# Expert 0's input by a gather of six tiles and one-hot products for the last two, with its first weights split ahead

## The chip, the cores and the metric

One core of one Trainium2 chip runs the whole layer. The metric is the device time of one launch in microseconds (us), taken as the median of several runs. Its engines are TensorE (PE; PEld is its weight load), VectorE (DVE), ScalarE (ACT), GpSimd (POOL) and SyncE (SP), which issues most transfers.

## What is computed

One decoder layer on 1024 tokens of width 1024, in float32:

```python
xn   = rms_norm(x, norm_mix_w)
proj = xn @ w_in                      # b, c, h, q, k, v, 512 columns each
yc   = conv group, ya = stick-breaking attention (8 heads x 64)
x    = x + concat([yc, ya]) @ w_out   # the "projection" of this text
xf   = rms_norm(x, norm_ffn_w)
g_idx = argmax(xf @ w_group + b_group)             # 4 groups
top_v, top_i = top_k(expert logits of that group, 2)   # 2 of 8 experts
gate = softmax(group)[g_idx] * softmax(top_v)
h    = silu(xf[rows of e] @ w1[e]) * (xf[rows of e] @ w3[e])
out[rows of e] += gate * (h @ w2[e])               # for each of 32 experts
```

## The kernel before

**Stages.** The mixer (input projection, convolution, attention) takes the first 420 us or so. Then come the projection with w_out, which also makes the normed rows and the routing tile by tile (a tile is 128 tokens, m = 0 to 7), then 32 rounds, one for each expert, and at the end the combination of the two experts' rows for each token.

**Precision.** Every large product runs as three float32r matmuls: an operand is split into `hi` (ACT or POOL rounds it) and `lo` (DVE subtracts), and PE sums hi*hi, hi*lo and lo*hi. For an expert's weights ACT makes `e_hi` in four pieces of 128x1024 (`act_split`, L1192 of the profile) and DVE makes `e_lo` (`dve_split`, L1198); `pe_product` uses a piece with six matmuls (L1161 to L1163).

**Projection.** For each tile PE multiplies two halves of 512 columns (`multiply`; `mixed` counts the halves), DVE adds them to the residual (`add`, L1693), ACT squares and takes roots (`square`), DVE scales (`scale`, for the last tile `scale_last` in two halves, L1707), and SP stores the normed tile in the DRAM array `xn2_rows`. PE turns the residual rows (`turn`, L1458), ACT or DVE copies them out (`x2T`; for the last half DVE at L1849), PE multiplies them with the router's weights (`route`, L1468), and DVE chooses groups and experts (`bias`, L1717, to `chosen`, L1774).

**Ranks and table.** The rank of each pair of token and expert among the expert's pairs comes from products of `chosen` with triangular and all-ones matrices (`count_before`, L1479 and L1481, and `count_all`), for tiles in the groups 0-3, 4-5, 6 and 7. `rank` (from L1782) turns them into slot and column; `one_hots` makes two one-hot matrices for each of 16 steps, and `table` (L1492) sums their products in PSUM: entry (slot, expert) is the token's number. `slots` (L1803) reads the table when all 16 steps are in. Blocks beyond 128 rows for one expert go on a list (`flag_blocks`, `list_blocks`).

**Rounds.** GpSimd gathers an expert's 128 rows from `xn2_rows` with an indirect DMA (L1244), PE turns them (`pe_turn_x`, L1150; for expert 0 `first_turn_x`, L1542), ACT and DVE make xT hi and lo (L1203 and L1208; for expert 0 in halves at L1632, L1634 and L1920). PE then does gate, up and, one round later, down. The order on each engine is that of the code. In round 0 PE does gate 0, then turns expert 1's rows, then up 0. ACT does W1[0], xT 0, the exponents, W3[0], xT 1, two pieces of W1[1], the silu of expert 0 and the other two pieces. PE's gate 1 waits for that silu. Between table and gate 0, PE runs 34 transposes of the identity that nobody reads (L1532 and L1536).

**Loads.** SP loads W1[0] during the projection, W3[0] when the last half is multiplied, and W1[1], W3[1], W2[0] when expert 0's rows have been gathered; each later load waits until DVE has made `lo` from the buffer it overwrites.

Of the kernel before, what the change touches and what calls it, by code (L numbers as in the profile page):

```python
# [44 lines left out]
def hymba_moe_layer(nc, x, norm_mix_w, w_in, conv_w, q_norm_w, k_norm_w, group_norm_conv_w,  # L45
# [34 lines left out]
    with ExitStack() as ctx:  # L80
# [967 lines left out]
        RANK_BANK = (3, 1, 3, 2)  # L1048
        TABLE, COUNT = 7, 1
# [29 lines left out]
        of_column = [place(f"of_column{i}", [P, COLS], F32R) for i in range(NOH)]  # L1079
        unused = at("unused", 160, [P, COLS])  # L1080
# [25 lines left out]
        over_ready = sem("over_ready")  # L1106
        gates_asked = sem("gates_asked")
# [15 lines left out]
        x1T_lo = at("x1T_lo", x1_kib + 4, [P, KT, P], F32R)  # L1123
        xT_of = lambda n: (x1T_hi, x1T_lo) if isinstance(n, int) and n == 1 else (xT_hi, xT_lo)
# [3 lines left out]
        e_lo = at("e_lo", 64, [P, PIECES, D], F32R)  # L1128
        idx_token = [keep(f"idx_token{i}", [P, 1], I32) for i in range(2)]
# [3 lines left out]
        def expert_sems(tag):  # L1133
# [3 lines left out]
                "gathered": [sem(f"{tag}_gathered{i}") for i in range(2)],  # L1137
                "scattered": [sem(f"{tag}_scattered{i}") for i in range(2)]}
# [14 lines left out]
        def pe_product(pe, s, start, xs_hi, xs_lo, out, per_piece, last, pieces=range(PIECES)):  # L1153

            for p in pieces:
                pe.wait_ge(s["lo_made"], start + p + 1)
                for j in range(D // BANK):
# [3 lines left out]
                    pe.matmul(o, xs_hi[:, k], e_hi[:, p, cols], start=(k == 0), stop=False)  # L1161
                    pe.matmul(o, xs_lo[:, k], e_hi[:, p, cols], start=False, stop=False)  # L1162
                    mm = pe.matmul(o, xs_hi[:, k], e_lo[:, p, cols], start=False, stop=(k == last))  # L1163
# [23 lines left out]
        def act_split(act, s, start, w, pieces=range(PIECES)):  # L1187
            flat = w.rearrange("p k f -> p (k f)")
            for p in pieces:

                act.wait_ge(s["freed"], start + p + 1)
                act.activation(e_hi[:, p], flat[:, p * D:(p + 1) * D], ACT.Copy).then_inc(s["hi_made"], 1)  # L1192

        def dve_split(dve, s, start, w, pieces=range(PIECES)):
            flat = w.rearrange("p k f -> p (k f)")
            for p in pieces:
                dve.wait_ge(s["hi_made"], start + p + 1)
                dve.tensor_tensor(e_lo[:, p], flat[:, p * D:(p + 1) * D], e_hi[:, p], ALU.subtract).then_inc(s["lo_made"], 1)  # L1198
# [43 lines left out]
        def gather_rows(pool, dst, rows, gathered):  # L1242
# [737 lines left out]
```

## Time and profile before

| what | us |
|---|---|
| median of 3 runs (1163.91 to 1165.25) | 1164.63 |
| the profiled execution's own time | 1164.24 |
| its span | 1162.1 |
| PE busy in the span | 1096.3 (94%) |
| DVE busy | 900.1 (77%) |
| ACT busy | 718.6 (62%) |
| first matmul of the projection | 409.0 |
| last matmul of the projection starts | 529.8 |
| first matmul of gate 0 | 550.4 |
| first matmul of gate 1 | 563.3 |
| last scatter issued | 1124.1 |

The profiled execution took 0.39 us less than the median, and 2.1 us of its time lie outside the span. Positions in the trace are us from the start of the span. Neighbouring matmuls overlap in the trace, so that the distance of their starts, not their duration, is what each costs.

### The profile page before, as it was taken

To read this page: it belongs to the slowest core of one execution; us is meant where nothing else is said; L and a number is where in the kernel's file an instruction comes from. 1 tells how busy PE (TensorE), PEld (TensorE's weight loads), DVE (VectorE), ACT (ScalarE), POOL (GpSimd) and SP (SyncE) were. 2 spreads that over 40 slices of the span, in tenths; PEclk is the share of its full clock that TensorE was granted. 3 is DMA by queue.
4 is the path that set the end of the run, shared out by engine and by line. 5 is a ranking of instruction groups with operands and counts; after the bars stand their busy time and mean duration, and the time that the engine had idled before them with its cause. 6 is when DMAs were issued, how large, how long until landed. Compare 5 with 4: busy or idle time off the path is not lost. (4 is left out here: it accounts for less than half of the span.)

```text
span 1162.1 us, 16798 instructions
## 1 busy us (share of the span) xinstructions
PE 1096.3 (94%) x5766; PEld 894.9 (77%) x5766; DVE 900.1 (77%) x1033; ACT 718.6 (62%) x882; POOL 139.7 (12%) x192
## 2 busy tenths in 40 slices
PE   8999999999999899997999999999999999999950
PEld 7887777778777668885878888888888888888840
DVE  5505957678575772567989999999999999999947
ACT  5423555646643571112878888888888888888830
POOL 1001000010000120001021110111111111101000
PEclk9999999999999999997999999999999999999985
DMA  7111231313213253003999999999999999999529
GB/s 232 46 35 39 90 89 59 107 39 107 67 46 95 103 214 142 37 37 133 425 427 422 396 384 396 386 384 396 382 383 390 382 392 383 390 387 387 214 77 375
DMA packets 77117, 275.29 MB, mean 237 GB/s; under 512 B 20752, under 2 KB 51600, under 8 KB 63888
## 3 DMA queue, kind: packets, MB, share of 16 engines
q1 hardware_dynamic: 66272, 253.69, 57.6%
q0 software_dynamic: 9216, 16.80, 3.8%
q10 hardware_dynamic: 1584, 4.20, 0.9%
q8 instruction: 29, 0.48, 0.2%
q14 instruction: 16, 0.13, 0.0%
HBM read 259.57 MB, written 31.85 MB: 251 GB/s over the span
## 5 line engine op out<-in xcount | busy, mean ns | idle before, releaser
L1198 DVE TENSOR_TENSOR e_lo<-W,e_hi 128x1024 fp32r<-128x1024 f32 x384 | 451.9, 1219 | 24.5 <-ACT e_hi L1192 21.7
L1192 ACT ACTIVATE e_hi<-W 128x1024 fp32r<-128x1024 f32 x384 | 403.4, 1060 | 94.7 <-PE ps L1163 88.7
L1161 PE MATMUL ps<-e_hi,xT_hi 128*128 128x512 f32 x496 | 196.3, 396 | 1.9 <-DVE xT_lo L1920 1.0
L1163 PE MATMUL ps<-e_lo,xT_hi 128*128 128x512 f32 x496 | 193.7, 390 | 0.0
L1162 PE MATMUL ps<-e_hi,xT_lo 128*128 128x512 f32 x496 | 193.1, 389 | 0.0
L472 PE MATMUL ps<-xnT_hi,w_hi 128*128 128x512 f32 x320 | 129.0, 403 | 1.6 <-DVE u L861 0.6
L472 PE MATMUL ps<-xnT_hi,w_lo 128*128 128x512 f32 x320 | 128.0, 400 | 0.0
L472 PE MATMUL ps<-xnT_lo,w_hi 128*128 128x512 f32 x320 | 125.3, 392 | 0.0
L900 DVE TENSOR_TENSOR_SCAN kept<-kept,start_at 128x1024 f32<-128x1024 f32 (+7 forms) x64 | 88.9, 1389 | 29.1 <-ACT kept L702 29.1
L1161 PEld LDWEIGHTS ps<-e_hi,xT_hi 128*128 128x128 f32 x496 | 93.5, 189 | 20.9 <-DVE xT_lo L1920 1.2
L1163 PEld LDWEIGHTS ps<-e_lo,xT_hi 128*128 128x128 f32 x496 | 93.1, 188 | 19.9
L1162 PEld LDWEIGHTS ps<-e_hi,xT_lo 128*128 128x128 f32 x496 | 93.3, 188 | 18.4
L1161 PE MATMUL ps<-e_hi,hidT_hi 128*128 128x512 f32 x256 | 102.4, 400 | 1.6 <-DVE hidT_lo L1232 1.6
L1163 PE MATMUL ps<-e_lo,hidT_hi 128*128 128x512 f32 x256 | 100.0, 390 | 0.0
L1162 PE MATMUL ps<-e_hi,hidT_lo 128*128 128x512 f32 x256 | 99.9, 390 | 0.0
L1259 POOL DMA_INDIRECT y_rows<-y,idx_pair x32 | 35.2, 1101 | 455.3 <-ACT y L1219 455.3
L711 ACT ACTIVATE probsT<-ps 128x512 f32<-128x512 f32 (+3 forms) x60 | 28.0, 504 | 84.1 <-PE ps L521 84.1
L472 PEld LDWEIGHTS ps<-xnT_hi,w_hi 128*128 128x128 f32 x320 | 60.1, 188 | 19.2 <-issue 7.1
L472 PEld LDWEIGHTS ps<-xnT_hi,w_lo 128*128 128x128 f32 x320 | 60.1, 188 | 13.0 <-issue 0.7
L472 PEld LDWEIGHTS ps<-xnT_lo,w_hi 128*128 128x128 f32 x320 | 60.1, 188 | 12.2 <-issue 0.5
L702 ACT ACTIVATE kept<-ps,q_minus 128x1024 f32<-128x1024 f32 (+7 forms) x64 | 47.8, 746 | 32.7 <-PE ps L510 32.6
L405 POOL CAST w_hi<-w_raw 128x1024 fp32r<-128x1024 f32 x20 | 22.4, 1120 | 301.4 <-DMA w_raw<-in_w_in_dram 301.4
(244 smaller groups left out, 1706.9 us busy)
## 6 DMA issues: line engine op xcount, KB each, us to landing
W<-in_w_dram SPq DMA_DIRECT2D x96, 2048.0 KB, 15.2
w_raw<-in_w_in_dram SPq DMA_DIRECT2D x20, 512.0 KB, 4.1
yy<-y_rows SPq DMA_DIRECT2D x7, 1024.0 KB, 12.7
xt<-in_x_dram SPq DMA_DIRECT2D x8, 512.0 KB, 3.7
w_out_raw<-in_w_out_dram SPq DMA_DIRECT2D x8, 512.0 KB, 6.4
xn_rows<-xn SPq DMA_DIRECT2D x8, 512.0 KB, 2.6
out_dram<-x ACTq DMA_DIRECT2D x7, 512.0 KB, 9.1
x<-in_x_dram SPq DMA_DIRECT2D x2, 1536.0 KB, 10.7
```

What stands on the lines that cost most here:

```text
L405: pool.tensor_copy(w_hi[c % 2], w_raw[c % 2]).then_inc(w_hi_made, 1)
L472: mm = pe.matmul(ps[:, group_bank(g)], w, r, start=(i % TICKS == 0), stop=(i % TICKS == TICKS - 1))
L702: act.activation(kept[h][:, S - L:], z, ACT.Sigmoid, scale=down).then_inc(kept_made, 1)
L711: act.activation(probsT[h][:, k0:k1, :], TB(th(n, h) + hf)[:, 0:(k1 - k0) * P].rearrange("p (k t) -> p k t", t=P), ACT.Copy).then_inc(turn ...
L900: dve.tensor_tensor_scan(back, back, one[:, ::-1], 0.0, ALU.mult, ALU.max).then_inc(multiplied, 1)
L1161: pe.matmul(o, xs_hi[:, k], e_hi[:, p, cols], start=(k == 0), stop=False)
L1162: pe.matmul(o, xs_lo[:, k], e_hi[:, p, cols], start=False, stop=False)
L1163: mm = pe.matmul(o, xs_hi[:, k], e_lo[:, p, cols], start=False, stop=(k == last))
L1192: act.activation(e_hi[:, p], flat[:, p * D:(p + 1) * D], ACT.Copy).then_inc(s["hi_made"], 1)
L1198: dve.tensor_tensor(e_lo[:, p], flat[:, p * D:(p + 1) * D], e_hi[:, p], ALU.subtract).then_inc(s["lo_made"], 1)
L1259: pool.indirect_dma_start(out=y_rows, out_offset=bass.IndirectOffsetOnAxis(ap=idx_pair[b].bitcast(U32), axis=0), in_=y[b], in_offset=None, ...
```

## The change

**Expert 0's rows.** The token list of expert 0 is made early. After `rank` of a group, DVE keeps `first_code`, 1 + the rank of a token for expert 0 (0 if it did not choose it), and `first_one_hots` makes a one-hot matrix for each tile. In tile 7 PE multiplies those of tiles 0 to 5 with the token numbers (`first_list`); DVE adds 2048 (slots that no such token fills stay out of bounds, and the destination was cleared) and GpSimd gathers from the first 768 rows. ACT and DVE split the gathered rows (`first_hi`, `first_lo`), and PE turns them by products with an identity in float32r (`first_gathered`), adding in the same PSUM banks the rows of tiles 6 and 7 by float32 products of `xn2` with their one-hot matrices (`first_added`). These banks are the transposed input of expert 0.

**Expert 0's gate weights.** W1[0] is split while the projection runs, into buffers of its own (`e0_hi`, `e0_lo`; `e0_lo` lies over W1[0] itself). ACT makes the four hi pieces after tile 5's work, DVE a lo piece in each of tiles 5, 6 and 7 and the last after xT lo.

**Order.** Both halves of `scale_last` stand ahead of the last `bias`. `rank(1)` moves from tile 7 to tile 6. The last four table steps move behind the third piece of gate 0, the exponents' operands (`ask_gates`) ahead of them, `slots` behind; picking and listing overflow blocks moves between the pieces of W3[0]. Expert 1's rows are turned behind up 0, no longer ahead of it. SP loads W1[1] without waiting, W3[1] once expert 1's rows are gathered, W1[2] once gate 0 has been multiplied. The 34 idle transposes go.

```diff
+                def first_list():
+                    bank, c0 = FIRST_AT
+                    pe.wait_ge(iotas, 12)
+                    pe.wait_ge(first_hots, NT - 2)
+                    for m in range(NT - 2):
+                        mm = pe.matmul(ps[:, bank, c0:c0 + 2], first_hot[:, m], token_less[:, m:m + 2], start=(m == 0), stop=(m == NT - 3))
+                    mm.then_inc(first_summed, 1)
+
+                def first_gathered(h):
+                    if h == 0:
+                        pe.wait_ge(iotas, 13)
+                        pe.wait_ge(rows0_lo_made, 1)
+                        pe.wait_ge(x2_made, 2 * NT)
+                    for k in range(4 * h, 4 * h + 4):
+                        o = psf[:, k * P:(k + 1) * P]
+                        pe.matmul(o, first_hi[:, k:D:KT], eye, start=(k % 4 == 0), stop=False)
+                        pe.matmul(o, first_lo[:, k:D:KT], eye, start=False, stop=False)
+
+                def first_added(m, ks):
+                    if ks[0] == 0:
+                        pe.wait_ge(first_hots, m + 1)
+                        pe.wait_ge(xn2_made, m + 1 + (m == NT - 1))
+                    for k in ks:
+                        mm = pe.matmul(psf[:, k * P:(k + 1) * P], xn2[m % 2][:, k:D:KT], HOT(m), start=False, stop=(m == NT - 1 and k % 4 == 3))
+                        if m == NT - 1 and k % 4 == 3:
+                            mm.then_inc(s_e["turned"] if k == KT - 1 else half_turned, 1)
...
                 turn(NT - 1, 1)
+                first_gathered(0)
                 route(NT - 1, 1)
+                first_gathered(1)
+                first_added(NT - 2, range(0, KT - 1))
                 count_before(3)
                 count_all()
-                table(12, 16)
-                for i in range(20):
-                    pe.transpose(ps[:, 4, 0:P], ident, ident)
-                pe.wait_ge(listed, 1)
-                pe.matmul(ps[0:1, 3, 0:P], over_col, ident, start=True, stop=True).then_inc(list_turned, 1)
-                for i in range(14):
-                    pe.transpose(ps[:, 4, 0:P], ident, ident)
...
+                first_added(NT - 2, (KT - 1,))
+                first_added(NT - 1, range(KT))
...
                     else:
+                        pe_product(pe, s_e, up_start(0), xT_hi, xT_lo, [ps[:, 3]], 2, KT - 1, (0, 1))
+                        overflow_list()
+                        pe_product(pe, s_e, up_start(0), xT_hi, xT_lo, [ps[:, 3]], 2, KT - 1, (2, 3))
+                        pe_turn_x(pe, s_e, 1, 1, 1)
+                        return
+                    if isinstance(e, int) and e == 1:
                         pe.wait_ge(over_ready, 1)
-                        pe_turn_x(pe, s_e, 1, 1, 1)
...
+                        if m == NT - 2:
+                            act.wait_ge(s_e["gathered"][0], 16)
+                            act.activation(first_hi, xg[0], ACT.Copy).then_inc(rows0_hi_made, 1)
+                        if m == 5:
+                            act.wait_ge(y_hi_made, Y_PARTS)
+                            act.wait_ge(y_lo_made, Y_PARTS)
+                            act.wait_ge(expert_w[0][0], 16)
+                            act_split(act, s_e, gate_start(0), W1[0], hi=e0_hi, free=True)
...
+                        dve_split(dve, s_e, up_start(0), W3[0], (0, 1))
+                        pick_blocks()
+                        dve_split(dve, s_e, up_start(0), W3[0], (2,))
+                        list_blocks()
+                        dve_split(dve, s_e, up_start(0), W3[0], (3,))
                         make_gates()
...
+                        dve_split(dve, s_e, gate_start(1), W1[1], (0,))
                         dve_xT(dve, s_e, 1)
-                        dve_split(dve, s_e, gate_start(1), W1[1], (0, 1))
+                        dve_split(dve, s_e, gate_start(1), W1[1], (1,))
                         dve_hid(dve, s_e, 0, up_start(0))
```

In the listings below `[waits ...]` names the semaphores that an instruction waits for. First PE at the end of round 0, before: the last matmul of gate 0, the transposes of expert 1's gathered rows (`xg_184`), the first matmuls of up 0.

```order
L1163 MATMUL ps<-e_lo,xT_hi 128x512
L1150 MATMUL ps<-start_at,xg_184 128x128 [waits first_xT_made,first_gathered1,over_ready]
L1150 MATMUL ps<-start_at,xg_184 128x128 x7
L1161 MATMUL ps<-e_hi,xT_hi 128x512 [waits first_lo_made,first_hidden]
L1162 MATMUL ps<-e_hi,xT_lo 128x512
```

With the change, the last matmul of up 0, the same transposes (`xg_188` now), the first matmuls of gate 1.

```order
L1181 MATMUL ps<-e_lo,xT_hi 128x512
L1168 MATMUL ps<-start_at,xg_188 128x128 [waits first_xT_made,first_gathered1]
L1168 MATMUL ps<-start_at,xg_188 128x128 x7
L1179 MATMUL ps<-e_hi,x1T_hi 128x512 [waits first_lo_made,first_silu,first_xT_made]
L1180 MATMUL ps<-e_hi,x1T_lo 128x512
```

The transposes stood between gate 0 and up 0 and now stand between up 0 and gate 1, whose operands come from them. Next DVE in round 0 with the change: the pieces of W3[0] (`W_0_104`), the picking of overflow blocks (to `over_col`) and their list (to `over_list`).

```order
L1216 TENSOR_TENSOR e_lo<-W_0_104,e_hi 128x1024 x2
L1964 SCALAR_TENSOR_TENSOR over_sel<-over_at,iota_p_129,over 128x224
L1965 TENSOR_TENSOR over_sel<-over_sel,iota 128x224
L1966 TENSOR_REDUCE over_col<-over_sel 128x1
L1216 TENSOR_TENSOR e_lo<-W_0_104,e_hi 128x1024
L1969 CAST over_n<-over_at 1x1
L1878 TENSOR_SCALAR unused<-ps 128x224
L1879 SCALAR_TENSOR_TENSOR slot_pair<-ps,unused 128x224
L1880 TENSOR_SCALAR slot_token<-slot_pair 128x224
L1974 CAST over_list<-ps 1x16
L1216 TENSOR_TENSOR e_lo<-W_0_104,e_hi 128x1024
L1982 TENSOR_REDUCE p_group<-e_178 128x8
```

Before, from the end of that list to the first pieces of W1[1] (`W_1_103`).

```order
L1877 CAST over_list<-ps 1x16
L1920 TENSOR_TENSOR xT_lo<-ps,xT_hi 128x512 x2
L1198 TENSOR_TENSOR e_lo<-W_0_102,e_hi 128x1024 x2
L1885 TENSOR_REDUCE p_group<-e_174 128x8
L1886 SCALAR_TENSOR_TENSOR gate_177<-e_diff,p_group 128x8
L1887 RECIPROCAL gate_177<-gate_177 128x8
L1888 TENSOR_TENSOR gate_178<-gate_177,e_diff 128x8
L1198 TENSOR_TENSOR e_lo<-W_0_104,e_hi 128x1024 x4
L1208 TENSOR_TENSOR x1T_lo<-ps,x1T_hi 128x1024
L1198 TENSOR_TENSOR e_lo<-W_1_103,e_hi 128x1024 x2
```

The four pieces of W3[0] stood in a row; now the bookkeeping stands between them. Last, PE with the change between the projection and gate 0: the last product of expert 0's gathered rows (`first_lo`), tile 6 (`xn_0_96`), the counts, tile 7 (`xn_1_97`), the first matmul of gate 0.

```order
L1537 MATMUL ps<-eye,first_lo 128x128
L1544 MATMUL ps<-last_hot,xn_0_96 128x128 [waits xn2_made,first_hots]
L1544 MATMUL ps<-last_hot,xn_0_96 128x128 x6
L1505 MATMUL ps<-chosen,before 128x32 [waits chosen_made,iotas]
L1507 MATMUL ps<-chosen,ones 128x32 x7
L1512 MATMUL ps<-chosen,ones 128x32 x8
L1544 MATMUL ps<-last_hot,xn_0_96 128x128
L1544 MATMUL ps<-last_hot,xn_1_97 128x128 [waits xn2_made,first_hots]
L1544 MATMUL ps<-last_hot,xn_1_97 128x128 x7
L1179 MATMUL ps<-e_hi,xT_hi 128x512 [waits first_lo_made,half_lo_made]
```


Tile 7's products follow the counts and gate 0 follows them; the table steps and the idle transposes that stood there are gone from this place.

## Rows read from the trace of the kernel before

**Rows 1.** PE's timeline, end of the projection to gate 1: start, us, work, idle time before.

```profile
529.78 0.40 PE L1312 MATMUL ps<-w_out_hi,yT_lo 128*128 128x512 f32 x1
...
538.19 0.18 PE L1479 MATMUL ps<-chosen,before 128*128 128x32 bf16 x1 [4.21 <-DVE chosen L1774]
...
541.70 4.47 PE L1532 MATMUL ps<-start_at 128*128 128x128 f32 x20
...
550.43 0.50 PE L1161 MATMUL ps<-e_hi,xT_hi 128*128 128x512 f32 x1 [0.97 <-DVE xT_lo L1920]
...
556.01 1.04 PE L1150 MATMUL ps<-start_at,xg 128*128 128x128 f32 x8
...
563.26 0.47 PE L1161 MATMUL ps<-e_hi,x1T_hi 128*128 128x512 f32 x1 [0.73 <-issue]
```

**Rows 2.** PE's waits, 550 to 1130 us: us in total, times, longest.

```profile
PE ps L1161 <- DVE e_lo L1198: 1.0, 1, 1.0
PE ps L1161 <- issue: 0.7, 1, 0.7
```

**Rows 3.** ACT's timeline, rounds 0 to 2.

```profile
557.18 1.01 ACT L1203 ACTIVATE x1T_hi<-ps 128x1024 fp32r<-128x1024 f32 x1
559.24 2.01 ACT L1192 ACTIVATE e_hi<-W 128x1024 fp32r<-128x1024 f32 x2 [1.05 <-DMA W<-in_w_dram]
...
565.26 2.08 ACT L1192 ACTIVATE e_hi<-W 128x1024 fp32r<-128x1024 f32 x2 [0.20 <-DMA W<-in_w_dram]
...
585.69 3.90 ACT L1192 ACTIVATE e_hi<-W 128x1024 fp32r<-128x1024 f32 x4 [2.40 <-DMA W<-in_w_dram]
```

**Rows 4.** DVE's timeline, tiles 6 and 7 of the projection.

```profile
514.58 0.69 DVE L1693 TENSOR_TENSOR x<-ps,x 128x512 f32<-128x512 f32 x1 [2.43 <-PE ps L1312]
...
518.22 0.47 DVE L1784 TENSOR_TENSOR ranked<-ps,of_expert 128x64 f32<-128x64 f32 x2
...
520.06 0.29 DVE L1797 TENSOR_SCALAR of_slot<-iota,slot 128x128 fp32r<-128x128 f32 x1
...
523.80 0.69 DVE L1693 TENSOR_TENSOR x<-ps,x 128x512 f32<-128x512 f32 x1
```

**Rows 5.** POOL's gather in the timeline; then its row of the DMA issues, us to landing.

```profile
543.66 1.46 POOL L1244 DMA_INDIRECT xg<-xn_rows,slot_token  x1 [38.90 <-issue]
...
xg<-xn_rows,slot_token POOLq DMA_INDIRECT x2, 4.6
```

**Rows 6.** DVE's timeline, from the last half tile to xT lo.

```profile
530.29 0.69 DVE L1693 TENSOR_TENSOR x<-ps,x 128x512 f32<-128x512 f32 x1
...
534.23 0.25 DVE L1717 SCALAR_TENSOR_TENSOR logits<-ps,rr,router_b 128x36 f32<-128x36 f32 x1
...
541.94 0.19 DVE L1803 TENSOR_SCALAR unused<-ps 128x32 f32<-128x32 f32 x1 [0.68 <-PE ps L1492]
...
543.56 0.45 DVE L1867 SCALAR_TENSOR_TENSOR over_sel<-over_at,iota_p,over 128x224 f32<-128x224 f32 x1
...
544.77 2.35 DVE L1198 TENSOR_TENSOR e_lo<-W,e_hi 128x1024 fp32r<-128x1024 f32 x2
...
547.22 0.13 DVE L1872 CAST over_n<-over_at 1x1 int32<-1x1 f32 x1
...
549.68 1.29 DVE L1920 TENSOR_TENSOR xT_lo<-ps,xT_hi 128x512 fp32r<-128x512 f32 x2 [1.04 <-ACT xT_hi L1632]
```

**Rows 7.** Stretches of PE: us, busy and instructions, granted clock (1.00 is full), DMA.

```profile
402.00:403.00 1.00, 0.59 (x6) 1.00 1.03 414
...
406.00:407.00 1.00, 1.00 (x18) 0.83 1.03 422
...
410.00:411.00 1.00, 1.00 (x5) 0.96 1.03 418
...
546.00:547.00 1.00, 1.00 (x6) 0.70 0.24 90
```

More of the change, by code:

```diff
@@ L1079, in hymba_moe_layer @@
         of_column = [place(f"of_column{i}", [P, COLS], F32R) for i in range(NOH)]
+        token_iota = place("token_iota", [P, NT])
+        token_less = place("token_less", [P, NT], F32R)
+        first_code = place("first_code", [P, NT])
+        first_token = place("first_token", [P, 1], I32)
         unused = at("unused", 160, [P, COLS])
@@ L1151, in pe_turn_x, with pe_product @@
             mm.then_inc(s["turned"], 1)
-        def pe_product(pe, s, start, xs_hi, xs_lo, out, per_piece, last, pieces=range(PIECES)):
+        def pe_product(pe, s, start, xs_hi, xs_lo, out, per_piece, last, pieces=range(PIECES), hi=e_hi, lo=e_lo):
             for p in pieces:
@@ L1185, in pe_down, with act_split, dve_split @@
             pe_product(pe, s, start, hidT_hi, hidT_lo, [ps[:, 5], ps[:, 6]], 1, FT - 1)
-        def act_split(act, s, start, w, pieces=range(PIECES)):
+        def act_split(act, s, start, w, pieces=range(PIECES), hi=e_hi, free=False):
             flat = w.rearrange("p k f -> p (k f)")
             for p in pieces:
-                act.wait_ge(s["freed"], start + p + 1)
-                act.activation(e_hi[:, p], flat[:, p * D:(p + 1) * D], ACT.Copy).then_inc(s["hi_made"], 1)
-        def dve_split(dve, s, start, w, pieces=range(PIECES)):
+                if not free:
+                    act.wait_ge(s["freed"], start + p + 1)
+                act.activation(hi[:, p], flat[:, p * D:(p + 1) * D], ACT.Copy).then_inc(s["hi_made"], 1)
+        def dve_split(dve, s, start, w, pieces=range(PIECES), hi=e_hi, lo=e_lo):
             flat = w.rearrange("p k f -> p (k f)")
@@ L1485, in count_all @@
                     for j in range(NT):
-                        mm = pe.matmul(ps[:, COUNT, 0:NE], ones, chosen[:, j], start=(j == 0), stop=(j == NT - 1))
+                        mm = pe.matmul(ps[:, COUNT_AT[0], COUNT_AT[1]:COUNT_AT[1] + NE], ones, chosen[:, j], start=(j == 0), stop=(j == NT - 1))
                     mm.then_inc(counted, 1)
@@ L1535, in _ @@
-                for i in range(14):
-                    pe.transpose(ps[:, 4, 0:P], ident, ident)
-                def first_turn_x():
-                    pe.wait_ge(s_e["gathered"][0], 16)
-                    for h in range(2):
-                        for k in range(4 * h, 4 * h + 4):
-                            mm = pe.transpose(psf[:, k * P:(k + 1) * P], xg[0][:, k:D:KT], ident)
-                        mm.then_inc(s_e["turned"] if h else half_turned, 1)
+                first_added(NT - 2, (KT - 1,))
@@ L1624, in round_of @@
                 def round_of(e, b, rounds, y_rounds=None, last=False):
-                    if not (isinstance(e, int) and e == 1):
+                    if not (isinstance(e, int) and e <= 1):
                         act.wait_ge(expert_w[b][0], 16 * rounds)
@@ L1774, in choose_experts, with first_one_hots @@
                     dve.tensor_tensor(chosen[:, ms], of_expert[:, 0, 0:w], of_expert[:, 1, 0:w], ALU.add).then_inc(chosen_made, 1)
+                def first_one_hots(first, last):
+                    for m in range(first, last):
+                        dve.tensor_scalar(HOT(m), iota[:, 1:P + 1], first_code[:, m:m + 1], None, ALU.is_equal).then_inc(first_hots, 1)
                 def rank(i):
```

146 lines of the change are left out of this document (97 added, 49 removed).

## The prediction

> **What bounds the kernel now.** I read the timelines first and the waits after them. The timeline of PE [rows 1] shows three things. The projection's last matmul starts at 529.78. Gate 0 starts at 550.43, 20.65 us later, and PE does little of use between. Gate 1 starts at 563.26, and from there PE is the bound: in the rest of the loop it waits for weights once, for 1.0 us [rows 2], because ACT waited 2.40 us for a load at 585.69 [rows 3]. So the end moves by as much as the start of gate 1 moves, less that 1.0 us if the load no longer comes late. The question is therefore not when gate 0 starts but when gate 1 does. Before, gate 1 waited for the silu of expert 0: ACT starts xT 1 at 557.18, then waits 1.05 us for W1[1], makes two pieces, loads a table and does the silu; the 0.73 us of idle PE before 563.26 end there [rows 1, 3].
>
> **The projection, part by part.** Three additions reach PE's path, which is full here.
> Tile 6: DVE had chosen 2.43 us before its addition at 514.58 [rows 4], at 512.15. Now `rank(1)` stands ahead of that addition. It waits for counts that PE makes some 0.9 us later and takes 1.84 us (520.06 less 518.22, rows 4) and 0.2 for `first_code`; two one-hots of 0.2 each follow. The addition comes at about 515.9, 1.3 us later. PE has some 0.8 us of other matmuls before it needs it, so that it waits 0.5.
> The list: six products of two columns, estimated at 0.1 each, 0.6 us.
> The gather: DVE's tile 7 now holds four more steps, two of them lo pieces of 1.14 (two started in 2.35 less overlap, rows 6), which put its first addition, at 523.80 before [rows 4], at 524.7, still ahead of PE's need. I put `first_token` at 521.8. Before, the slots were written at 542.56 (0.62 after 541.94, rows 6), GpSimd issued at 543.66, and the rows landed 4.6 us later [rows 5]: 5.7 us in all, hence 527.5. ACT waits for it ahead of `x2T` of tile 7, and needs 1.06 for `first_hi` and 0.6 for `x2T`: 529.2. PE arrives there at about 528.6 and waits 0.6, with the last six projection matmuls behind it.
> Together 1.7 us: the last addition, at 530.29 before [rows 6], comes at 532.0. DVE's own work (`first_lo` at 528.6, then rank and one-hot of tile 6) ends at 531.8, so it sets nothing. The unread cost is the gather: had it landed at issue, 0.6 us less; had it taken 3 us more, 3 more.
> The DMA page of the Trainium skill (DMA: Bandwidth & Descriptors, section on the anatomy of one GpSimd DMA) puts such a transfer at 2.0 us and its bytes over 436 GB/s, an estimate of 3.2 us for these 512 KB, against 4.6 in this trace. By it the sum would be 0.5 us lower.
> The hi pieces on ACT (4 of about 1 us, in tile 5) and the first lo piece cost nothing: ACT waits for PE afterwards, and DVE has over 2 us of idle time in tile 5 as in tile 6 [rows 4]. Without that idle time the piece would cost its 1.14.
>
> **From the last addition to gate 0.** From it to `bias` 3.94 (534.23), from there to the count 3.96 (538.19), and from there to the end of rank and two pairs of one-hots 3.07 (541.94 less 0.68 idle) [rows 1, 6]. New are `first_code` and the last one-hot, 0.45. xT lo to PE takes 0.75 (550.43 less 549.68). Sum 12.2. The products of tile 7 end under the one-hots, if the clock is full. Moved out of the way: table steps, slots, the idle transposes (4.47 us for the first 20, rows 1), the gather with its 5.7 us, two lo pieces. Gate 0 starts at 544.2, 6.2 us earlier. This is the gain.
>
> **From gate 0 to gate 1.** Before, 12.83 us (563.26 less 550.43, rows 1). Now a chain: three pieces of gate 0 at 1.40 (556.01 less 550.43, over four, rows 1), 4.2; four table steps and a hand-over, 0.8; slots, 0.6; four lo pieces of W3[0] at 1.14, 4.6; among them picking, 1.2 (544.77 less 543.56), and listing, 1.4 (from 547.22 on) [rows 6]. At 12.8 the last lo piece is there. PE needs 1.40 for it, then turns expert 1's rows: 1.17 from the first transpose to ACT's xT 1 (557.18 less 556.01) [rows 1, 3]. ACT's xT 1, two pieces, table load and silu need 563.26 less 557.18 less 1.05 of waiting, 5.0. Sum 20.4, which is 7.6 more than before. Gate 1 starts at 564.6, **1.3 us later**. Before, xT 1 and the pieces lay under up 0; that cover is gone, since the transposes now stand behind up 0. W1[1] left 12 us earlier and is no longer late. Expert 1's gather, issued at about 551, has landed by 555.5, ahead of PE at 558.4.
>
> **Loads.** W3[1], W2[0], W1[2] and W2[1] now leave at about 555.5, when that gather lands. Five loads remain to land where before there were six, so the load that came 2.40 us late [rows 3] comes hardly late: 1.0 us back. At full clock the end moves by +0.3.
>
> **The clock.** PE stood idle for 3.2 us from 402.6 on; its granted clock was at 0.5, 1.2 GHz, from within 406 to 407 until within 410 to 411 [rows 7]. That is 3.9 us at half speed, which costs 1.9 us of dense work. Between the end of expert 1's transposes and gate 1 PE now idles for 5.0 us, so I charge 1.9 there. Ahead of gate 0 the idle transposes were what brought 2.4 GHz back, at 546.6, 4.9 us after they began [rows 1, 7]. They are gone; the small products in their place leave PE free for half of the time from 532 on. The bounds are nothing and 3.4 us (4.9 us at half speed in gate 0, and 0.9 for the products of tile 7). I take 1.5, since the products begin 3 us before gate 0. Sum: +0.3 +1.9 +1.5 = +3.7. The profiled execution took 1164.24, so 1168.0, and since the median stands 0.39 above it, **1168.4**.
>
> **The rivals.**
> B, the clock falls only once, at the end of round 0, because the products with the identity and the one-hots keep PE awake until gate 0. For it: some 30 new matmuls lie there. Against: before, it fell within that stretch. +2.2, 1166.9.
> C, the clock holds at both places: 1164.63 +0.3, 1165.0. The 5 us of idle PE speak against it.
> D, the gain lives: **faster**. Place: the end of round 0. If xT 1, two pieces and the silu still cost only what they did before, because up 0 ends early enough, the 6.2 us stay: 1158.4. It decides at the end of up 0: the end moves forward by over 2.3 us if PE has turned expert 1's rows by 556. The order on PE speaks against it, and the chain of 12.8 us on DVE.
> E, the four loads of 2048 KB that leave together share the queues, and W3[1], needed from about 566, lands with the others. Before, three that left within 1 us served ACT one after another, at 559.24 and 565.26 [rows 3], which speaks against it. The first still took 11 us, so W3[1] lands near 566 with no room. Shared, it comes about 4 us late on PE's path: 1172.4.
> On this the same page of the Trainium skill (section on queues, rings and completion order) says that completion is not in order of issue in general; the trace shows it in order for those, and no run here shows another case.
>
> **How the numbers follow.** Chances: forecast 0.42 (its own range 1166.9 to 1170.2), B 0.22, C 0.12, D 0.14, E 0.10. A measurement of this kernel tells 0.2%, 2.3 us, from no change: the limits are 1162.3 and 1167.0. Faster is D, 0.14. Slower is E, nine tenths of the forecast and half of B, 0.59. The rest, 0.27, is the same. The range runs from 1164.4, below C, to 1171.0, which takes in a gather later by 2.6 us; it leaves out D and about half of E.
>
> **What would show it.** In the profile after: last addition near 532; gate 0 near 544; gate 1 near 564.6 at full clock, near 566 otherwise, with 5 us of idle PE before it that end at ACT; a granted clock of 0.5 in it. Up 0 should wait for DVE's lo pieces three times. The wait of 1.0 us at about 586 should be gone. I am wrong if gate 1 starts before 562, or if PE waits for a load in round 1.

## The result, and the profile after

The changed kernel took 1171.82 us (median of five runs, 1168.89 to 1172.42), the kernel before 1164.88 on the same chip (five runs, 1163.91 to 1166.65). The ratio is 1.0055, with an interval of 1.004 to 1.0071. A second measurement of the same two kernels on another chip gave 1168.79 and a ratio of 1.0038 (1.0025 to 1.0051). Slower, as forecast, and in the first measurement 0.8 us above the top of the range.

The profiled execution took 1168.89 us, its span is 1167.2. These are the rows that answer to [rows 1]: PE's timeline (start, us, work, idle time before and what ended it).

```profile
517.93 0.66 PE L1483 MATMUL ps<-start_at,x 128*128 128x128 f32 x4 [0.39 <-DVE x L1760]
...
532.38 0.40 PE L1330 MATMUL ps<-w_out_hi,yT_lo 128*128 128x512 f32 x1
...
534.24 0.40 PE L1537 MATMUL ps<-eye,first_lo 128*128 128x128 f32 x1
534.48 0.40 PE L1536 MATMUL ps<-eye,first_hi 128*128 128x128 f32 x1
...
535.93 1.03 PE L1493 MATMUL ps<-router_w,x2T 128*128 128x36 f32 x8
536.79 0.43 PE L1536 MATMUL ps<-eye,first_hi 128*128 128x128 f32 x1
...
538.74 3.66 PE L1544 MATMUL ps<-last_hot,xn 128*128 128x128 f32 x14
...
542.19 0.23 PE L1505 MATMUL ps<-chosen,before 128*128 128x32 bf16 x1
...
542.66 4.60 PE L1544 MATMUL ps<-last_hot,xn 128*128 128x128 f32 x18
547.02 0.47 PE L1179 MATMUL ps<-e_hi,xT_hi 128*128 128x512 f32 x1
...
553.87 0.50 PE L1179 MATMUL ps<-e_hi,xT_hi 128*128 128x512 f32 x1 [0.65 <-DVE e_lo L1216]
559.82 0.51 PE L1179 MATMUL ps<-e_hi,xT_hi 128*128 128x512 f32 x1 [0.81 <-DVE e_lo L1216]
...
561.32 1.04 PE L1168 MATMUL ps<-start_at,xg 128*128 128x128 f32 x8
...
567.38 0.77 PE L1179 MATMUL ps<-e_hi,x1T_hi 128*128 128x512 f32 x1 [5.02 <-ACT act_out L1232]
```

DVE's timeline, the rows that answer to [rows 4, 6]:

```profile
517.19 0.68 DVE L1760 TENSOR_TENSOR x<-ps,x 128x512 f32<-128x512 f32 x1
...
522.89 0.15 DVE L1901 TENSOR_SCALAR first_token<-ps 128x1 int32<-128x1 f32 x1
...
525.74 0.69 DVE L1760 TENSOR_TENSOR x<-ps,x 128x512 f32<-128x512 f32 x1
...
532.82 0.69 DVE L1760 TENSOR_TENSOR x<-ps,x 128x512 f32<-128x512 f32 x1 [0.37 <-PE ps L1330]
...
540.62 0.19 DVE L1841 TENSOR_TENSOR chosen<-of_expert 128x32 bf16<-128x32 f32 x1
542.64 0.16 DVE L1853 SCALAR_TENSOR_TENSOR first_code<-ps,chosen 128x1 f32<-128x1 f32 x1 [1.83 <-PE ps L1507]
```

ACT's timeline at the end of round 0, as [rows 3]:

```profile
562.46 1.02 ACT L1221 ACTIVATE x1T_hi<-ps 128x1024 fp32r<-128x1024 f32 x1 [7.33 <-PE ps L1168]
563.38 1.99 ACT L1210 ACTIVATE e_hi<-W 128x1024 fp32r<-128x1024 f32 x2
565.39 1.28 ACT L1232 ACT_TABLE_LOAD   x1
566.68 0.60 ACT L1232 ACTIVATE act_out<-ps 128x512 f32<-128x512 f32 x1
```

Stretches of PE (us, busy of PE, weight loads, DVE, ACT and GpSimd with their instructions, granted clock, DMA share, GB/s), as [rows 7]:

```profile
534.00:546.00 12.00, 12.00 (x71) 11.94 (x68) 8.30 (x34) 1.53 (x4) 0.00 (x0) 0.72 0.95 380
...
538.00:544.00 6.00, 6.00 (x39) 5.94 (x40) 3.59 (x20) 0.00 (x0) 0.00 (x0) 0.50 1.02 410
...
564.00:571.00 7.00, 3.62 (x9) 2.88 (x10) 6.36 (x6) 5.76 (x7) 1.79 (x2) 0.53 1.02 425
```

Put side by side, the two profiled executions part as follows. The projection's first matmul starts at 410.31, before at 409.05. The profile of the second measurement is later still, at 411.81. This is not the change's doing: where it happens, PE's granted clock stood at 0.5 for some microseconds near 12 us into the span, in code that the change does not touch (in the second measurement near 129 us as well), and among the kernels below this comes and goes (it is in the profiles of e7 and e10).

| stretch | before | after | difference | forecast |
|---|---|---|---|---|
| start to the projection's first matmul | 409.05 | 410.31 | +1.26 | 0 |
| to the last addition | 121.24 | 122.51 | +1.27 | +1.7 |
| to gate 0 | 20.14 | 14.20 | -5.94 | -7.9 |
| gate 0 to gate 1 | 12.83 | 20.36 | +7.53 | +7.6, and 1.5 for the clock |
| gate 1 to expert 0's first down product | 12.30 | 14.16 | +1.86 | +1.9 |
| from there to the end | 586.59 | 585.62 | -0.97 | -1.0 |

Without the first line the spans (1162.14 and 1167.16 us) differ by 3.76 us, and the forecast's own sum is 3.7. The composition is another: the 1.5 us for a slow gate 0 did not come, 2.0 us that the sum did not have stand ahead of gate 0, and the projection took 0.4 less.

The last line of the table holds two things. From expert 0's first down product to expert 2's, two rounds on, it is 36.98 us before and 35.50 after: the load that came late costs 1.5 us there. From expert 2's to PE's last product it is 509.7 us in every profile here. Behind PE's last product it is 39.9 us before and 40.4 after, and 39.6 to 41.0 among all profiles, without a pattern that the edits explain. So what loads cost is read below from those two rounds.

### The profile page after: what moved, and what is told of

Read it like the earlier page. It is cut to its first block and busy times, and to the rows that moved or that the text cites. A ratio compares the mean times of both kernels' runs of the same rounds, so it can differ in the third digit from the quotient of the medians.

```text
span 1167.2 us, 16845 instructions
## 1 busy us (share of the span) xinstructions
PE 1103.2 (95%) x5778; PEld 902.6 (77%) x5778; DVE 904.8 (78%) x1047; ACT 718.7 (62%) x883; POOL 139.5 (12%) x195
## 5 line engine op out<-in xcount | busy, mean ns | idle before, releaser
L1277 POOL DMA_INDIRECT y_rows<-y,idx_pair x32 | 32.6, 1019 | 456.6 <-ACT y L1237 456.6
```

What stands on the lines that cost most here:

```text
L1277: pool.indirect_dma_start(out=y_rows, out_offset=bass.IndirectOffsetOnAxis(ap=idx_pair[b].bitcast(U32), axis=0), in_=y[b], in_offset=None, ...
```

## The experiments

Every kernel was timed against the kernel before on its own chip. It gave 1164.07 us beside e1 to e4 (26 runs), 1165.29 beside e5 to e8 (18), 1164.25 beside e9 to e11 (24), 1163.63 beside e12 (15) and 1164.16 beside e13 (13), so ratios are compared, not times. A is the last addition, as in the prediction.

**e1, the change once more.** No edit.

> The changed kernel once more, unaltered. Its five runs fell into two groups, 1169 and 1172. Theory 1 (the granted clock decides between them, by where it falls and comes back ahead of gate 0 and gate 1): again a spread of some 3 us, and a profile whose stretch from the last addition to gate 1 at half speed is as long as its time is high: at 1172 about 6 us more of half speed than the 6.4 us before gate 0 and 6.7 around gate 1 of the first profile. Theory 2 (the groups come from transfers): the same half-speed time, and a load that PE waits for.

Measured: 1168.79 (1168.04 to 1171.99), ratio 1.0038 (1.0025 to 1.0051). Its profiled execution, the slowest, 1171.99, has A to gate 0 14.74, gate 0 to gate 1 20.38, gate 1 to the first down product 15.03. Between it and the first profile lie 3.1 us of the same kernel. 1.5 lie before the projection, with one more stretch of half clock near 129 us. 0.9 lie at gate 1: the stretch of half clock there is 6.8 us long in both, but in this profile it ends 5.8 us after gate 1's start, in the first 3.9. 0.5 lie ahead of gate 0: the router's eight products in the middle of the products with the identity fell into half clock here and took 1.45 us (537.62 to 539.07), in the first profile 0.86. Theory 1 is right in that the clock decides, but the half clock ahead of gate 0 and around gate 1 is as long as in the first profile, not 6 us longer; it lies elsewhere. No load is waited for, so theory 2 is out. Single executions of this kernel differ by about what the change costs.

**e2, expert 1's rows turned inside up 0.** The cover that the change took away is given back in part:

```
-pe_product(pe, s_e, up_start(0), ..., (2, 3))
+pe_product(pe, s_e, up_start(0), ..., (2,))
 pe_turn_x(pe, s_e, 1, 1, 1)
+pe_product(pe, s_e, up_start(0), ..., (3,))
```

> Alone: PE turns expert 1's rows between the third and the fourth piece of up 0, where it waited 0.8 us for DVE anyway, instead of behind the fourth. Theory 1 (the serial chain behind those transposes, 5.0 us of idle PE, is what the gain of gate 0 is paid back with): the transposes come 2.4 us earlier, gate 1 starts 2.2 to 2.5 us earlier, PE's wait before it falls from 5.0 to about 2.6, and the median falls by 2 to 3 us, more if the clock then holds. Theory 2 (PE is cold and slow there anyway, or loads bound round 1): under 1 us.

Measured: 1166.39 (10 runs), ratio 1.0019 (1.001 to 1.0029). Gate 0 to gate 1 is 17.9 us instead of 20.4, and PE idles 3.45 before gate 1 (2.6 were expected). But ACT waits 1.83 for W3[1] at 566.87, and PE 0.82 for pieces at 589.60: the two rounds take 36.9 us, not 35.5, so 1.4 of the gain go to loads.

**e3, PE kept busy at the boundary.** 36 idle transposes between expert 1's transposes and gate 1.

> Alone: 36 transposes of the identity, read by nobody, stand between expert 1's transposes and gate 1, where PE was idle for 5.0 us. Theory 1 (part of the loss is gate 1 at 1.2 GHz, about 4 us at half speed): the granted clock stays at 1.00 through gate 1, the start of gate 1 stays, and the time falls by 1.5 to 2 us. Theory 2 (the clock costs nothing there, since the later loads had to be waited for anyway): 0, and waits for loads appear.

Measured: 1167.33 (9 runs), ratio 1.0026 (1.0016 to 1.0035). Gate 0 to gate 1 is 20.36 as before the edit; the granted clock stays at full, and gate 1 to the first down product is 12.28, not 14.16. That is the 1.9 us of the prediction, seen alone. But PE waits 0.48 us for pieces at 590.12 again, and the two rounds take 36.5 us, not 35.5: half of the 1.9 goes to loads. The ratio is 1.2 thousandths below that of e1, with intervals that overlap.

**e4, the kernel before without its 34 idle transposes.**

> The kernel before, without its 34 idle transposes between table and gate 0. It prices a cold gate 0 apart from all else. Theory 1 (without them gate 0 starts at 1.2 GHz): gate 0 starts when it did, its first matmuls are 0.43 us apart until the clock is back after 3 to 5 us, and the time rises by 1.5 to 2.5 us. Theory 2 (the chain of loads and ACT sets gate 1, and hides it): gate 1 starts no later, under 0.5 us.

Measured: 1165.47 (12 runs), ratio 1.0012 (1.0003 to 1.0021). PE is at half clock from 535 to 556, and gate 0 to gate 1 takes 14.6, not 12.83. A cold gate 0 does cost 1.8 us at gate 1, in the kernel before; the two rounds then take 35.5 us instead of 37.0, since the wait of 1.0 us for a load is gone. In the changed kernel gate 0 is not cold in the first profile.

**e5, the gathered rows turned by fp32 products.** Eight instead of sixteen, with the same step; ACT's `first_hi` and DVE's `first_lo` go, and PE waits for the gather instead of `first_lo`. Parts of the edit:

```
-pe.matmul(o, first_hi[:, k:D:KT], eye, start=(k % 4 == 0), stop=False)
-pe.matmul(o, first_lo[:, k:D:KT], eye, start=False, stop=False)
+pe.matmul(o, xg[0][:, k:D:KT], ident, start=(k % 4 == 0), stop=False)
...
-act.activation(first_hi, xg[0], ACT.Copy).then_inc(rows0_hi_made, 1)
...
-dve.tensor_tensor(first_lo, xg[0], first_hi, ALU.subtract).then_inc(rows0_lo_made, 1)
```

> The gathered rows of expert 0 are turned by 8 fp32 products with an fp32 identity, not by 16 fp32r products with hi and lo pieces; ACT's first_hi and DVE's first_lo go with them. Theory 'the products with the identity were mis-sized and are on the path': the 16 start 0.24 us apart in the profile of the changed kernel, 3.8 us, and hold count_before(3) until 1.4 us after DVE has chosen. Eight of about 0.25 take 2.0: the count comes 1.4 us earlier, and without first_hi ahead of x2T the last addition 0.6 to 1.0 earlier. Last addition to gate 0: 12.8 (14.2 before). Gate 0 to gate 1 stays 20.4. Time 1166.4 to 1167.2. Rival, 'the products are hidden under DVE's steps, as the prediction had it': only the 0.6 of the last addition, 1168.2, and gate 0 still 14.2 after the last addition.

Measured: 1168.19 (7 runs), ratio 1.003 (1.0019 to 1.0041). A miss for the theory's numbers: A to gate 0 14.02 and the last addition 122.7 after the projection's first matmul, both as in the change. The PE rows say why: four fp32 products take from 533.21 to 535.11, 0.48 us each, so that eight cost what sixteen had. And ACT's `first_hi` ahead of `x2T` cost PE nothing.

**e6, the products with the identity twice.** Expert 0's gathered rows count double.

```
 pe.matmul(o, first_lo[:, k:D:KT], eye, start=False, stop=False)
+pe.matmul(o, first_hi[:, k:D:KT], eye, start=False, stop=False)
+pe.matmul(o, first_lo[:, k:D:KT], eye, start=False, stop=False)
```

> Each product with the identity is done twice (32, not 16; expert 0's gathered rows count double in what is computed, all else the same). Theory 'mis-sized and on the path': 16 more at 0.24 is 3.8 us on PE ahead of count_before(3), nothing hides them; last addition to gate 0 18.0, gate 0 to gate 1 20.4, time 1172.6. Rival 'hidden, about 0.1 each': 1.6 us of work under DVE's steps, 0 to 0.6 on the path, 1168.8 to 1169.4.

Measured: 1173.36 (6 runs), ratio 1.0072 (1.0058 to 1.0086); A to gate 0 18.84, gate 0 to gate 1 20.37. "Hidden, 0.1 each" is out: sixteen more products cost 4.64 us, all on the path. The products themselves are 0.24 apart as before, 3.8 us. The other 0.8 is the clock's: the router's eight products between them now fall into half clock and take 1.67 us, where they took 0.86 in the change.

```profile
536.40 1.86 PE L1493 MATMUL ps<-router_w,x2T 128*128 128x36 f32 x8
538.07 0.46 PE L1536 MATMUL ps<-eye,first_hi 128*128 128x128 f32 x1
```

**e11, the one-hot products of tile 6 left out.** Its rows are missing from expert 0's input.

```
-first_added(NT - 2, range(0, KT - 1))
 count_before(3)
 count_all()
-first_added(NT - 2, (KT - 1,))
```

> The eight one-hot products of tile 6 are left out (the rows of tile 6 are missing from expert 0's input), all else as changed. Theory 'PE is full between the last addition and gate 0, with DVE's chain close behind': the products take 0.49 us each, two profile records, 3.9 us in all; without them the count comes as soon as DVE has chosen (540.8 instead of 542.2 in the profile of the changed kernel), tile 7's one-hot 1.4 earlier, its eight products end 1.4 earlier: last addition to gate 0 12.8 (14.2), time 1.4 us below the changed kernel. Rival, 'only PE's work counts': 3.9 us less, 10.3. Rival, 'only DVE's chain counts, as the prediction had it': no change, 14.2.

Measured: 1167.92 (7 runs), ratio 1.0032 (1.002 to 1.0044); A to gate 0 12.93 for 12.8 expected. PE then waits 2.02 us for DVE ahead of the count. So DVE's chain stands only some 1.3 us behind PE's queue here. It did not all reach the end: in this profile the first products of gate 0 ran at half clock (0.43 us apart), and gate 0 to gate 1 took 21.45.

**e13, why these products are dear.** The columns of the stationary operand side by side, not every eighth; expert 0's input has its columns in another order.

```
-pe.matmul(o, first_hi[:, k:D:KT], eye, ...)
-pe.matmul(o, first_lo[:, k:D:KT], eye, ...)
+pe.matmul(o, first_hi[:, k * P:(k + 1) * P], eye, ...)
+pe.matmul(o, first_lo[:, k * P:(k + 1) * P], eye, ...)
...
-mm = pe.matmul(psf[...], xn2[m % 2][:, k:D:KT], HOT(m), ...)
+mm = pe.matmul(psf[...], xn2[m % 2][:, k * P:(k + 1) * P], HOT(m), ...)
```

> The changed kernel, with the 128 columns of the stationary operand of the identity and one-hot products taken side by side in SBUF, not every eighth (expert 0's input has its columns in another order, so its output is another; all counts, loads and steps are the same). In the profiles so far the weight loads of these products last 331 to 338 ns and follow each other without a gap, 0.24 us a product, where those of the dense work last 188. Theory 'the weight load with a step of 8 is the price': loads of 188 ns or less, products 0.13 us apart for fp32r, 0.26 for a one-hot; PE needs some 6 us for all, not 11.6, DVE no longer waits for the count, and last addition to gate 0 is 12.2 to 12.9, as the prediction had it: 1.3 to 2.0 less than the changed kernel, ratio 1.002 to 1.003. Rival 'the price is that of the type (fp32r and fp32 words), not of the step': weight loads still 331 to 338 ns, 14.2, ratio 1.0038.

Measured: 1166.97 (8 runs), ratio 1.0025 (1.0014 to 1.0036); A to gate 0 11.81, below the 12.2 to 12.9 expected. The groups of weight loads from the last addition to gate 0 (busy us, mean ns of one, idle before), first of the changed kernel:

```profile
L1544 PEld LDWEIGHTS ps<-last_hot,xn 128*128 128x128 f32 x32 | 7.9, 335 | 0.0
L1537 PEld LDWEIGHTS ps<-eye,first_lo 128*128 128x128 f32 x8 | 2.7, 338 | 0.0
L1536 PEld LDWEIGHTS ps<-eye,first_hi 128*128 128x128 f32 x8 | 2.6, 331 | 0.0
```

then with a step of one:

```profile
L1544 PEld LDWEIGHTS ps<-last_hot,xn 128*128 128x128 f32 x32 | 3.8, 192 | 0.2 <-DVE last_hot L1845 0.2
L1537 PEld LDWEIGHTS ps<-eye,first_lo 128*128 128x128 f32 x8 | 1.5, 192 | 0.0
L1536 PEld LDWEIGHTS ps<-eye,first_hi 128*128 128x128 f32 x8 | 1.5, 192 | 0.0
```

and PE's timeline there, where the products now stand 0.11 us apart:

```profile
533.35 0.28 PE L1537 MATMUL ps<-eye,first_lo 128*128 128x128 f32 x1
533.47 0.28 PE L1536 MATMUL ps<-eye,first_hi 128*128 128x128 f32 x1
...
535.85 1.78 PE L1544 MATMUL ps<-last_hot,xn 128*128 128x128 f32 x14
539.55 0.18 PE L1505 MATMUL ps<-chosen,before 128*128 128x32 bf16 x1 [1.93 <-DVE chosen L1841]
...
543.64 0.50 PE L1179 MATMUL ps<-e_hi,xT_hi 128*128 128x512 f32 x1 [1.11 <-DVE xT_lo L1886]
```

Its stretch there:

```profile
533.00:545.00 12.00, 8.90 (x81) 8.06 (x79) 10.23 (x37) 3.48 (x6) 0.00 (x0) 1.00 0.96 375
```

Nothing but the step was changed, so for these products the step is the price. Without it PE waits for DVE twice (1.93 and 1.11 us), and gate 0 comes 11.8 after A: the chain that the prediction had priced at 12.2. Of these 2.4 us, 0.85 are lost at gate 1 in this profile (15.01 to the first down product, for 14.16), where the half clock lies later.

The rival "the type is the price" is out, but the step does not cost every instruction as much. The transposes of expert 1's rows in the changed kernel read the same kind of rows with the same step (`pe.transpose(..., xg[b][:, k:D:KT], ident)`), and there the weight load is short:

```profile
L1168 PEld LDWEIGHTS ps<-start_at,xg 128*128 128x128 f32 x8 | 1.0, 188 | 0.1
```

Eight of them take 1.0 us. Why a transpose is spared was not tried.

**e7, the end of round 0 shortened.** The fp32 products and the turn inside up 0 of above; silu 0 on ACT right behind W3[0]'s hi pieces, and xT 1 behind two pieces of W1[1]; the gates' steps (`make_gates`) on DVE behind W1[1]. ACT's part of the edit:

```
 act_split(act, s_e, up_start(e), W3[b], ...)
...
-act.wait_ge(s_e["freed"], used(gate_start(0) + PIECES))
-act_xT(act, s_e, 1)
+act_silu(act, s_e, 0, gate_start(0))
 act.wait_ge(expert_w[1][0], 16)
 act_split(act, s_e, gate_start(1), W1[1], (0, 1))
-act_silu(act, s_e, 0, gate_start(0))
+act_xT(act, s_e, 1)
```

> The fp32 products of the first kernel here, and the end of round 0 shortened: expert 1's rows turned between the third and fourth piece of up 0, silu 0 on ACT right behind the hi pieces of W3[0] (ahead of W1[1] and xT 1), the gates' four small steps on DVE behind W1[1]. Theory 'a chain at the end of round 0': gate 0 to gate 1 16.2 us (17.9 with the turn alone, 20.4 unchanged), no half-speed stretch behind gate 1, gate 1 some 6 us earlier than in the changed kernel. Theory 'the loads give back': W3[1] and all that follow it leave when gather 1 has landed, 2.1 us earlier than before and no more, so the end moves only by that from the 1166.4 of the turn alone: 1163.6 to 1164.6, with PE waiting for loads 2 to 4 us in round 1. Rival, loads do not bind: 1160.5 to 1162.0 without such waits.

Measured: 1168.87 (6 runs, 1165.98 to 1170.69), ratio 1.0036 (1.0022 to 1.005): no gain over the 1.003 of the fp32 products alone, and slower than the 1163.6 to 1164.6 forecast. The profile is of the fastest execution, 1165.98, 2.9 us below the median, and can explain that one alone. In it the chain is shorter: gate 0 to gate 1 15.26, gate 1 to the first down product 12.54 at full clock, together 6.7 us less than in the change. But the two rounds from there take 38.9, against 35.5, so 3.4 of the 6.7 are given back to loads (and 0.6 behind PE's last product). ACT waits four times for weights and PE last (PE's waits, 550 to 1130 us: in total, times, longest):

```profile
PE ps L1179 <- DVE e_lo L1216: 3.3, 3, 2.5
```

What the median execution loses beyond this, no profile shows.

**e8, W3[1] leaves with the gather of expert 1.** As e7. In SP's list its wait for that gather's landing becomes a wait for the slots:

```
-sp.wait_ge(s_e["gathered"][1], 16)
+sp.wait_ge(routed, 1)
 sp.dma_start(W3[1], w3_v[1]).then_inc(expert_w[1][1], 16)
```

> As the third kernel here, and W3[1] leaves when DVE has written the slots of expert 1, not when its rows have landed: about 4 us earlier, beside the gather. Theory 'the loads give back': 2 to 3 us faster than the third kernel, 1161 to 1162. Rival, 'the gather is slowed by the load beside it': the rows of expert 1 land 3 us or more later, PE waits for them ahead of the last piece of up 0, and the time is that of the third kernel or above it.

Measured: 1167.45 (12 runs), ratio 1.0022 (1.0012 to 1.0032). The rival came true in the profile: the gather, issued at 552.25, takes 10.5 us beside W3[1], which left at 551.32, and three more loads from 555.97 on, and PE stands for the rows inside up 0, so that gate 0 to gate 1 takes 21.45 us. The other theory shows as well: the two rounds behind the first down product take 35.8 us, not 38.9. PE's timeline, and the gather's row of the DMA issues (us to landing):

```profile
562.82 1.97 PE L1168 MATMUL ps<-start_at,xg 128*128 128x128 f32 x8 [5.11 <-DMA xg<-xn_rows,slot_token]
...
xg<-xn_rows,slot_token POOLq DMA_INDIRECT x1, 10.5
```

**e9, W3[1] leaves before the gather.** As e7, with that wait deleted, so that W1[1] and W3[1] leave at 536 us.

```
 sp.dma_start(W1[1], w1_v[1]).then_inc(expert_w[1][0], 16)
-sp.wait_ge(s_e["gathered"][1], 16)
 sp.dma_start(W3[1], w3_v[1]).then_inc(expert_w[1][1], 16)
```

> As e7_short_and_fp32, but W3[1] leaves right behind W1[1], 20 us earlier, when the queues are empty, and not beside or behind the gather of expert 1's rows. Theory 'the loads give back': e7 lost 3.9 us after its first down product (589.6 to the end, against 585.7 where PE never waits for a load); here gate 0 to gate 1 stays 15.3, the first down product to the end is 585.7 to 586.2, PE waits for no load at 589, and the ratio to before falls from 1.0036 to 1.0005 or below, 1164 to 1165.5. The gather of expert 1 lands within 4.5 us of its issue, since both loads have landed before it. Rival, 'the queues are full from the start of the loop, whatever leaves first': the next loads come late instead, and the 589 stays.

Measured: **1162.04** (12 runs, 1161.35 to 1164.22), ratio **0.9983** (0.9972 to 0.9995): faster than both kernels, and than the 1164 to 1165.5 expected. PE's timeline, the gather, and PE's waits from 550 to 1130 us:

```profile
545.84 0.47 PE L1179 MATMUL ps<-e_hi,xT_hi 128*128 128x512 f32 x1
...
561.09 0.50 PE L1179 MATMUL ps<-e_hi,x1T_hi 128*128 128x512 f32 x1 [0.79 <-DVE x1T_lo L1226]
...
xg<-xn_rows,slot_token POOLq DMA_INDIRECT x1, 4.4
...
PE ps L1179 <- DVE hidT_lo L1250: 1.6, 1, 1.6
PE ps L1179 <- DVE x1T_lo L1226: 0.8, 1, 0.8
PE ps L1179 <- DVE e_lo L1216: 0.6, 1, 0.6
```

The two rounds from the first down product (573.62) take 35.8 us: 3.0 of the 3.4 us that e7 gave back to loads are kept. That is 2.6 of the 5.3 thousandths between the two ratios. The two profiles differ by 4.6 us in all, 1.1 of it before the projection, by the stretch of half clock near 12 us; what the ratios differ by beyond that lies between e7's profile and its median.

**e10, e2 with W3[1] first.** The edits of e2 and e9 in the changed kernel.

> As e2_turn_inside, and W3[1] leaves right behind W1[1]. e2 waited 1.83 us of ACT's time at 566.9 and 0.82 of PE's at 589.6 for loads. Theory 'the loads give back': both waits gone, first down product to the end 585.7 to 586.2 (587.0 in e2), 1 us faster than e2: ratio 1.001, 1165.5. Rival, 'W3[1] was never late enough to matter': as e2.

Measured: 1166.34 (12 runs), ratio 1.0014 (1.0004 to 1.0024), against 1.0019 (1.001 to 1.0029). Both load waits are gone, and the two rounds from the first down product (578.90) take 35.5 us, 1.4 less than in e2's profile, as expected. But the 0.5 thousandths between the ratios lie inside their intervals.

**e12, e9 with the fp32r products back.**

> As e9_w3_first, but the gathered rows of expert 0 are turned by the 16 fp32r products with hi and lo pieces again, as in the change. In the profiles so far each run with those products has a stretch of 6.8 to 10.2 us at half the granted clock ahead of gate 0 (from about 536 on), each run with 8 fp32 products has none. Theory 'products of 128 columns do not feel the clock' (0.24 us apart at either level): the half-speed stretch of about 6.8 us comes back, last addition to gate 0 stays 14.0 to 14.2, gate 0 to gate 1 15.3, and the time is within 1 us of e9: ratio 0.998 to 0.9995. Rival, 'the clock costs half of the stretch': 3.4 us more, ratio 1.001 and gate 0 17.4 after the last addition.

Measured: 1161.69 (11 runs), ratio 0.9987 (0.9978 to 0.9996). The stretch of half clock is back (PEclk of 534 to 546 is 0.72, and 1.00 in the kernel with fp32 products), and A to gate 0 is 14.21, gate 0 to gate 1 15.27. In these numbers it costs nothing.

## Why the prediction was right or wrong

**Right: the sign and the place.** Gate 0 comes earlier and gate 1 does not, because a chain of 20.4 us replaces one of 12.83. The forecast of that chain, 20.4, was met to 0.1 (20.36), with 5.0 us of idle PE before gate 1 ended by the silu. DVE's last lo piece is there 12.8 us after gate 0 (559.82), as priced; up 0 waited for DVE twice, not three times. The turn alone gave 2.5 of it back, the reordered ACT and the rest 2.6 more. The load that no longer comes late gives back 1.5 us in the two rounds, for 1.0.

**Right by luck: 1.9 us for the clock at gate 1.** It is 1.86 in the first profile, and idle transposes bring it to zero (e3). But the figure came from a stretch taken as 3.9 us at half speed, and a mean clock of 0.83 in its first microsecond and 0.96 in its last [rows 7] make it 3.4. Around gate 1 the stretch was 6.8 us, of which 3.9 happened to lie behind gate 1's start. In the second profile of the same kernel 5.8 did, and the cost was 2.7 us.

**Right in sum, not in parts: the projection.** Counted from the projection's first matmul, tile 6's addition comes at 515.93 (forecast 515.9), tile 7's first at 524.48 (524.7), `first_token` at 521.63 (521.8); the gather landed 4.0 us after its issue, not 4.6. The steps that the prediction lists for tile 6 add up to 515.5, not 515.9; what they lack is the wait for the counts, 1.33 us and not 0.9. PE's wait there is 0.39 for 0.5, and the list's products take 0.59 (520.50 to 521.09) for 0.6. The last addition is later by 1.27, not 1.7. The 0.6 for ACT blocked by `first_hi` was wrong: without `first_hi` the addition comes no earlier (122.54 us after the projection's first matmul in e9, 122.50 in e12 with it).

**Wrong: "The products of tile 7 end under the one-hots, if the clock is full."** This step gave the 16 products with the identity and the 16 with the one-hots no term in the sum; it took that they leave PE free for half of the time and lie under DVE's steps. They stand 0.24 and 0.49 us apart, 11.6 us in all: an fp32r product has a weight load of 331 to 338 ns (means) with a step of 8, a one-hot product in fp32 two of them. From 534 to 546 PE is busy for 12.00 of 12 us, and its weight loads for 11.94. The count waits 1.4 us behind them after DVE has chosen, and the last nine one-hot products take 4.4. A to gate 0 was 14.20, not 12.2; with unit steps it is 11.81.

**Wrong: 1.5 us for the clock in gate 0.** The granted clock did fall, from within 536 to 538 until about 544, with PE busy throughout, but in the stretch of products with a step of 8, which keep their 0.24 us, and was back for gate 0. So the clock cost what rival B says, though not for B's reason. Of the profiles of kernels with the change only e11's has gate 0 start at half clock, for about 1 us more. The 2.0 us too little for the products, the 1.5 too much for the clock and the 0.4 too much for the projection cancel by luck, and the sum against one profile was 3.76 for 3.7.

**Wrong: the range's top.** This, and not the terms above, put the median outside: the first profile took 1168.89, 0.9 above the 1168.0 forecast for it, but the median lay 2.93 us above that profile, not 0.39. The range was built from bounds of the terms on one profiled execution of before. It had nothing for how far executions of the changed kernel differ: 1168.04 to 1172.42 over ten, with a median of 1171.82 in the first five and 1168.79 in the second. Between its two profiles, 3.1 us apart, 1.5 us lie before the projection, where one has a second stretch of half clock near 129 us, 0.9 at gate 1 and 0.5 ahead of gate 0, all three by where half clock falls. Of the first five executions the three near 1172 us had a mean granted clock of 0.973 to 0.975 over the span, the two near 1169 us 0.976 and 0.977. What brings such stretches on in one execution and not in another stays open.

**The rivals.** D, with the gain alive, said that the end of round 0 decides. It does: with PE turning expert 1's rows inside up 0 and the silu ahead of them, gate 1 follows gate 0 after 15.3 us. But half of it was given back, and the median showed none of it, until the load behind it left earlier. E, loads late by 4 us, did not occur in the change: they came late only when gate 1 was made earlier.

## What to carry to other kernels

A gain ahead of a boundary is kept only if two things move with it: the chain behind the boundary, and the loads that it releases. Here, with 6.7 us off the chain, 3.4 went back to loads while W3[1] left after a gather, and the ratio was 1.0036; it was 0.9983 once W3[1] left before. And look up what a small product's weight load takes, with the step of its stationary operand, before calling the product hidden: here 0.24 us with a step of 8, 0.11 without.

## What was not expected of the hardware

- A weight load of 128x128 whose columns are 8 words apart lasted 331 to 338 ns on average, side by side 192 (e13). The fp32r products followed each other 0.24 and 0.11 us apart. In a transpose with the same step of 8 it lasted 188 ns.
- Such products with a step of 8 do not feel the granted clock: 0.24 us apart in the full-clock stretch before 536 us, 0.24 in the half-clock one after 538. Others beside them do: the 512-column products of the dense work go from 0.23 to 0.43 (e11), the router's eight products, whose stationary columns lie side by side, from 0.86 to 1.67 us (e6). The Trainium skill (TensorE: Matmul & The Clock Gate, section "Wait — 56ns, not 53.3ns?") gives 56 ns and 107 ns between bf16 products of 128 columns at the two clocks; no run here has such a product. Its fp32r ones of 128 columns stood 0.24 us apart with a step of 8 and 0.11 side by side, at the full clock.
- The clock fell ahead of gate 0 in all eight profiles with fp32r products of step 8 there (from about 537 to 544 in the changed kernel), though PE was idle in that stretch in e11 alone. It fell there in none of the four with eight fp32 products in their place, and not in e13 with unit steps, where PE was busy for only 8.90 of 12 us. What sets this apart was not tried.
- A gather of 512 KB landed 4.4 us after its issue with little else under way (e9; the DMA share was 0.28 from 549 to 552 us and 0.20 from there to 556), and 10.5 us after it beside a load of 2048 KB that had left 0.9 us earlier and three more that followed (e8). The Trainium skill (DMA: Bandwidth & Descriptors, section "Queues, rings and completion order") says that a DMA engine takes turns between its queues packet by packet. The slower gather is in keeping with that but does not show it: one that had to wait behind the load would be late too.
